# Attention scores of a two-block forward pass: from one f32 product to two f32r products over rounded halves

## The reference

```python
h = rms_norm(x, norm_mix_w[layer]); proj = h @ w_in[layer]
q_nsa = rope(...); k_slc = rope(kv[:, :, 2], ...); k_win = rope(kv[:, :, 4], ...)
kc = gelu(blk(k_cmp) @ w1) @ w2                      # 15 compressed keys for each group
s_cmp = einsum('bshgd,bchd->bhgsc', qg, kc) * scale  # masked softmax, times compressed values
s     = einsum('bqhgd,bhqnkd->bhgqnk', qb, kg) * scale   # selected blocks
s_win = einsum('bnqhgd,bnkhd->bnhgqk', qb, kb) * scale   # window
o = g[..., 0:1] * o_cmp + g[..., 1:2] * o_slc + g[..., 2:3] * o_win
```

## Time and profile before

| what | value |
|---|---|
| median of 3 runs | 1285.89 us (1285.88 to 1286.3) |
| time of the profiled execution | 1286.23 us |
| its span in the trace | 1284.9 us |
| PE busy | 1273.1 us, 99% of the span |
| DVE, ACT, POOL busy | 69%, 53%, 28% |
| share of PE in the chain that ended last | 95% |
| granted clock of PE | 1.00 in every stretch read |

### The profile page before, as it was taken

The page is one execution under the profiler, slowest core; times in us unless marked ns, Lnnn a source line. Parts: engine busy times, 40 slices in busy tenths (PEclk is TensorE's granted clock), DMA queues, the critical chain, the costliest instruction groups (busy, mean ns, idle before and its releaser), DMA issues.

```text
span 1284.9 us, 20030 instructions
## 1 busy us (share of the span) xinstructions
PE 1273.1 (99%) x8220; PEld 1150.0 (90%) x8220; DVE 890.5 (69%) x1309; ACT 686.7 (53%) x985; POOL 356.7 (28%) x268
## 2 busy tenths in 40 slices
PE   8999999999999999999999999999999999999999
PEld 6988889989999879899998888888999998888887
DVE  6775565768888468985567777646898476877752
ACT  6644445466655355466746555435456674655541
POOL 0110021014440059476450000007857733000000
PEclk9999999999999999999999999999999999999999
DMA  9653233555555546734364555544854444555551
GB/s 353 252 193 135 99 116 136 193 183 194 175 188 192 191 147 235 233 134 157 137 212 164 197 183 180 193 164 172 270 196 139 157 157 172 192 174 191 195 186 45
DMA packets 36572, 230.77 MB, mean 180 GB/s; under 512 B 4480, under 2 KB 5120, under 8 KB 10496
## 3 DMA queue, kind: packets, MB, share of 16 engines
q1 hardware_dynamic: 36480, 229.48, 50.9%
HBM read 222.12 MB, written 1.05 MB: 174 GB/s over the span
## 4 chain that ended last, share of the span: by engine, by line
PE 95%; DVE 2%; ACT 1%; DMA 1%; POOL 1%; issue 0%; SPq 0%; DVEq 0%; POOLq 0%
PE ps L601 13%; PE ps L580 12%; PE ps L582 12%; PE ps L581 12%; PE ps L521 11%; PE ps L523 11%; PE ps L522 11%; PE ps L602 7%; PE ps L526 6%; PE ps L540 1%; PE ps L992 1%; PE ps L754 0%; DMA raw<-in_w 0%; POOL sg L1622 0%; DMA gnw<-in_rows 0%
## 5 line engine op out<-in xcount | busy, mean ns | idle before, releaser
L1080 ACT ACTIVATE whi<-raw 128x2048 fp32r<-128x2048 f32 x205 | 390.2, 1906 | 170.9 <-PE ps L523 100.5
L1725 DVE TENSOR_TENSOR wlo<-raw,whi 128x2048 fp32r<-128x2048 f32 (+1 forms) x165 | 380.1, 2307 | 137.7 <-ACT whi L1080 137.1
L580 PE MATMUL ps<-hh,whi 128*128 128x256 f32 x992 | 283.6, 286 | 0.0
L582 PE MATMUL ps<-hh,wlo 128*128 128x256 f32 x992 | 280.6, 283 | 0.0
L581 PE MATMUL ps<-hh,whi 128*128 128x256 f32 x992 | 280.5, 283 | 0.0
L601 PE MATMUL ps<-hh,whi 128*128 128x512 f32 x704 | 249.3, 399 | 0.0
L1601 POOL TENSOR_TENSOR wlo<-raw,whi 128x512 fp32r<-128x512 f32 x160 | 203.8, 1306 | 135.5 <-ACT whi L1080 132.4
L602 PE MATMUL ps<-hh,wlo 128*128 128x256 f32 x704 | 197.7, 281 | 0.0
L581 PEld LDWEIGHTS ps<-hh,whi 128*128 128x128 f32 x992 | 190.1, 192 | 0.4 <-issue 0.2
L580 PEld LDWEIGHTS ps<-hh,whi 128*128 128x128 f32 x992 | 190.0, 192 | 0.4 <-issue 0.2
L582 PEld LDWEIGHTS ps<-hh,wlo 128*128 128x128 f32 x992 | 190.0, 192 | 0.0
(11 more groups left out here) (304 smaller groups left out, 2088.6 us busy)
## 6 DMA issues: line engine op xcount, KB each, us to landing
raw<-in_w SPq DMA_DIRECT2D x203, 1024.0 KB, 4.8
raw<-in_w SPq DMA_DIRECT2D x8, 256.0 KB, 6.4
kst<-kh SPq DMA_DIRECT2D x16, 128.0 KB, 2.4
qst<-qh SPq DMA_DIRECT2D x16, 128.0 KB, 2.3
raw<-in_w SPq DMA_DIRECT2D x2, 560.0 KB, 15.9
x<-in_x SPq DMA_DIRECT2D x2, 512.0 KB, 4.9
gain<-in_rows SPq DMA_DIRECT2D x2, 512.0 KB, 10.2
kst<-kl SPq DMA_DIRECT2D x8, 128.0 KB, 2.4
```

Source lines behind the costliest of these rows:

```text
L580: pe.op.matmul(o, wh[:, k, c:c + 128], hi[:, k, :], start=first, stop=False, skip_group_check=True)
L582: ins = pe.op.matmul(o, wl[:, k, c:c + 128], hi[:, k, :], start=False, stop=last, skip_group_check=True)
L1080: act.op.activation(t.whi[i % NHI][:, 0:n], t.raw[i % NRAW][:, 0:n], ACT.Copy).then_inc(*at("act_hi", ("hi", i)))
L1725: dve.op.tensor_tensor(t.wlo[i % NRAW][:, c], t.raw[i % NRAW][:, c], t.whi[i % NHI][:, c].bitcast(F32), ALU.subtract).then_inc(*at("dve_lo ...
```

## The change

Queries and keys are rounded to f32r halves. For each head the 64 upper rows of the queries stand over the 64 lower ones (`qs`, turned to `q1`); the keys of a group stand twice, one copy above the other (`kd`), turned, and split into `k1h` (upper) and `k1l` (lower). Two f32r products over 128 contraction rows, with `k1h` and with `k1l`, then give all four partial products. The same is done with the compressed keys (`kcs`), where the results of upper and lower keys lie beside each other and DVE adds them. POOL copies the keys twice instead of zeroing `kT`. The weights `w2k` stand twice (64 KB more in a table).

The core of the diff:

```diff
-    ("w2k", 128), ("w2v", 128), ("pe", 32), ("fconv", 4 * 2 * NFT),
+    ("w2k", 256), ("w2v", 128), ("pe", 32), ("fconv", 4 * 2 * NFT),
...
     g = rows("qr", *h)
     steps(g, 5)
-    for tt in range(2):
-        turned(("qT", tt), [("q roped", tt)], t.qkv[tt][:, 0:512], 4)
+    def q_turned(tt):
+
+        src = t.qs[tt][:, :, :, :].rearrange("p h a d -> p (h a d)").bitcast(F32)
+        for h in range(2):
+            turned(("qT", tt, h), [("q lo", tt)], src[:, half(h)], 4)
+
+    q_turned(0)
     run(g)
+    q_turned(1)
...
-    for tt in range(2):
+    def k_turned(tt):
+
         b = take_bank(("kT", tt))
-        pe.wait_ge(*on("k roped", tt))
-        for j in range(2):
-            ins = pe.op.transpose(t.pb[b][:, j * 128:j * 128 + 128], t.qkv[tt][:, 768 + 256 * j:896 + 256 * j], ident)
+        pe.wait_ge(*on("k twice", tt))
+        for gr in range(2):
+            for j in range(2):
+                ins = pe.op.transpose(t.pb[b][:, (2 * gr + j) * 128:(2 * gr + j) * 128 + 128],
+                                      t.kd[tt][:, gr, j, :, :].rearrange("p a d -> p (a d)"), ident)
...
-            product(t.sc[1][gr * 64:gr * 64 + 64, 0:15], w2[0][:, hf, :], t.Hg[:, 0, hf, gr * 15:gr * 15 + 15],
-                    hf == 0, hf == 1, [("kc",)] * (gr + hf == 2))
+            product(t.sc[1][:, gr * 16:gr * 16 + 15], w2[0][:, hf, :],
+                    t.Hg[:, 0, hf, gr * 15:gr * 15 + 15], hf == 0, hf == 1, [("kc",)] * (gr + hf == 2))
...
         product(t.tp[0:120, 0:64], t.Hr[:, hf, :], w2[1][:, hf, :], hf == 0, hf == 1, [("vc",)] * (hf == 1))
+    for tt in range(2):
+        k_turned(tt)
     run(g)
...
-        for b in range(4):
-            product(t.sc[0][:, b * 32:b * 32 + 32], t.qT[:, b, tok(tt)], t.kcT[:, :, :],
-                    names=[("cmp scores", tt)] * (b == 3))
+        for j in range(8):
+            product(t.sc[0][:, j * 32:j * 32 + 32], t.q1[:, j, tok(tt)], t.kcs[:, :, j % 2, :],
+                    names=[("cmp scores", tt)] * (j == 7))
...
-        product(bk[:, :].rearrange("p (a k) -> p a k", a=2)[:, :, 0:n], t.qT[:, b, tok(tt)], t.kT[:, gr, :, 0:n],
-                True, False)
+        for k in t.k1h, t.k1l:
+            product(bk[:, :].rearrange("p (a k) -> p a k", a=2)[:, :, 0:n], t.q1[:, 2 * b + gr, tok(tt)],
+                    k[:, gr, :, 0:n], k is t.k1h, False)
...
+    for tt in range(2):
+        upper(("q hi", tt), t.qs[tt][:, :, 0, :], t.qkv[tt][:, 0:512].rearrange("p (h d) -> p h d", h=8), ("q roped", tt))
     act.wait_ge(*on("gates copied", 1))
...
+    for tt in range(2):
+        lower([("q lo", tt)], t.qs[tt][:, :, 1, :], t.qkv[tt][:, 0:512].rearrange("p (h d) -> p h d", h=8),
+              t.qs[tt][:, :, 0, :], ("q hi", tt))
     run(rows("qr", rotated("qr")))
...
+    for tt in range(2):
+        lower([("free", ("kT", tt))], t.k1l[:, :, :, tok(tt)],
+              bank(("kT", tt))[:, :].rearrange("p (g a s) -> p g a s", g=2, a=2), t.k1h[:, :, :, tok(tt)],
+              ("k hi", tt))
     run(g)
...
         for gr in range(2):
-            dve.op.tensor_tensor(t.cs[:, gr * 4:gr * 4 + 4, :],
-                                 t.sc[0][:, 0:128].rearrange("p (b g c) -> p b g c", g=2, c=16)[:, :, gr, 0:15],
-                                 bc(madd, [128, 4, 15], 1), ALU.add).then_inc(
+            s = t.sc[0][:, 0:256].rearrange("p (b g a c) -> p b g a c", g=2, a=2, c=16)[:, :, gr, :, 0:15]
+            part = t.cs[:, gr * 4:gr * 4 + 4, :]
+            dve.op.tensor_tensor(part, s[:, :, 0, :], bc(madd, [128, 4, 15], 1), ALU.add).then_inc(*at("dve_small"))
+            await_own()
+            dve.op.tensor_tensor(part, s[:, :, 1, :], part, ALU.add).then_inc(
                 *at("dve_small", *([("cmp masked", tt)] * gr)))
```

More of the change, by code:

```diff
@@ L314, in place @@
     t.qkv = [at(f"qkv{i}", n0 + 5.25 * i, [128, 1304]) for i in range(2)]
-    t.qT = at("qT", n0 + 10.5, [128, 4, S])
-    t.kT = at("kT", n0 + 30.5, [128, 2, 2, S])
-    t.Ex = [at(f"Ex{i}", (n0 + 16.5, n0 + 18.5, n0 + 80)[i], [128, 2, S]) for i in range(3)]
+    t.qs = [at(f"qs{i}", n0 + 41 + (12, 20)[i], [128, 8, 2, 64], R32) for i in range(2)]
+    t.kd = [at(f"kd{i}", n0 + (14.5, 26.5)[i], [128, 2, 2, 2, 64]) for i in range(2)]
+    t.q1 = at("q1", p, [128, 8, S], R32)
+    t.k1h, t.k1l = (at(n, n0 + a, [128, 2, 2, S], R32) for n, a in (("k1h", 10.5), ("k1l", 30.5)))
+    t.Ex = [at(f"Ex{i}", n0 + (16.5, 18.5, 14.5)[i], [128, 2, S]) for i in range(3)]
     t.ET = [at(f"ET{i}", n0 + 20.5 + 2 * i, [128, 4, 128]) for i in range(2)]
@@ L713, in compressed @@
     def compressed(tt):
-        pe.wait_ge(*on("qT", 0))
-        pe.wait_ge(*on("qT", 1))
-        pe.wait_ge(*on("kcT"))
+        for k in range(2):
+            pe.wait_ge(*on("free", ("qT", k, 1)))
+        pe.wait_ge(*on("kc lo"))
         if tt:
             pe.wait_ge(*on("exp", 6))
-        for b in range(4):
-            product(t.sc[0][:, b * 32:b * 32 + 32], t.qT[:, b, tok(tt)], t.kcT[:, :, :],
-                    names=[("cmp scores", tt)] * (b == 3))
+        for j in range(8):
+            product(t.sc[0][:, j * 32:j * 32 + 32], t.q1[:, j, tok(tt)], t.kcs[:, :, j % 2, :],
+                    names=[("cmp scores", tt)] * (j == 7))
         yield
@@ L1215, in act_program, with q_turned_out @@
     steps(g, 5)
-    for tt in range(2):
-        turned_out(("qT", tt), t.qT[:, :, tok(tt)])
+    def q_turned_out(tt):
+        for h in range(2):
+            turned_out(("qT", tt, h), t.q1[:, 4 * h:4 * h + 4, tok(tt)])
+    q_turned_out(0)
     run(g)
+    q_turned_out(1)
     def ret_turned(w, tt):
@@ L1230, in act_program @@
             *at("act_small", ("gelu", kv)))
-    run(rows("kr"))
+    g = rows("kr")
+    steps(g, 1)
+    upper(("kc hi",), t.kcs[:, 0, :, 0:15], t.sc[1][:, 0:32].rearrange("p (g c) -> p g c", g=2)[:, :, 0:15], ("kc",),
+          ("rest zero",))
+    for tt in range(2):
+        upper(("k hi", tt), t.k1h[:, :, :, tok(tt)],
+              bank(("kT", tt))[:, :].rearrange("p (g a s) -> p g a s", g=2, a=2), ("kT", tt))
+    run(g)
     units = [(tt, hd) for tt in range(2) for hd in range(8)]
@@ L1607, in pool_program @@
         norm_power("n0", tt)
[L1608 to L1612, removed]
+    for tt in range(2):
+        pool.wait_ge(*on("k roped", tt))
+        for gr in range(2):
+            k = t.qkv[tt][:, 768:1280].rearrange("p (j g d) -> p j g d", j=2, g=4)[:, :, gr, :]
+            pool.op.tensor_copy(t.kd[tt][:, gr, :, :, :], bc(k, [128, 2, 2, 64], 2)).then_inc(
+                *at("pool_small", *([("k twice", tt)] * gr)))
     for w in ("qr", "kr"):
@@ L1948, in dve_program @@
         splits(i + AHEAD)
[L1949 to L1953, removed]
     kr = UNITS["kr"]
@@ L1962, in dve_program @@
             *at("dve_small", *([("Hr",)] * hf)))
-    for gr, rows_of in enumerate(groups):
-        copied([("kcT",)] * gr, t.kcT[rows_of, gr, 0:15], t.sc[1][rows_of, 0:15], ("kc",), ("rest zero",))
+    lower([("kc lo",)], t.kcs[:, 1, :, 0:15], t.sc[1][:, 0:32].rearrange("p (g c) -> p g c", g=2)[:, :, 0:15],
+          t.kcs[:, 0, :, 0:15], ("kc hi",))
     splits(kr[1])
@@ L2561, in _small @@
     put("bm", (np.arange(120)[:, None] // 15 == np.arange(8)[None, :]).astype(f))
-    put("w2k", a["cmp_w2_k"][0].reshape(2, 128, 64).transpose(1, 0, 2))
+    put("w2k", np.tile(a["cmp_w2_k"][0].reshape(2, 128, 1, 64), (1, 1, 2, 1)).transpose(1, 0, 2, 3))
     put("w2v", a["cmp_w2_v"][0].reshape(2, 128, 64).transpose(1, 0, 2))
```

7 lines of the change are left out of this document (3 added, 4 removed).

## The result

The change made the kernel slower: median 1290.66 us (1290.31 to 1291.9, 6 runs) against 1285.92 us (1285.87 to 1286.3, 6 runs), a ratio of 1.0035 with a 95% interval of 1.0025 to 1.0045, or +4.7 us. The prediction said +2.6, and its range of 1285.3 to 1290.7 holds the result by 0.04 us. The profiled execution took 1290.9 us, its span is 1289.6. What is in the profile of after stands two or more lines lower in the program: L542 turns blocks, L523 to L525 are `mul3`, L739 turns `cp`, L768 the probabilities.

The account below looks back on a forecast made before the run. PE, busy 99% of the span, was taken to set the end. Gain -3.9, added work +1.7 and waits +4.75 made +2.6 us: 1288.8 us, or 1288.5 against the median; 8-in-10 range 1285.3 to 1290.7.

Parts of the forecast that it names:

- rival 2: DVE slips: POOL's key copies slow the queries' subtraction, which ends 2.8 us late; sum +5.4, 1291.3 us; chance 10%.
- The gain in the scores: Heads' scores on PE get cheaper, 0.19 us each in the first token tile, 0.40 in the second; 3.9 us in all.
- The last two heads pay nothing: Heads 14 and 15, second tile: shorter scores only lengthen PE's wait behind DVE, by 0.8 us.
- More work on PE: Eight more query transposes +0.9 us, four more key transposes +0.4, wider compressed keys' product +0.4; sum +1.7 us.
- (A): After `qr`, PE waits to turn the second tile's queries until DVE frees the `qr` banks; 2.85 us (2.0 to 3.4).
- (B): The second tile of `vr0` takes a bank of `kr`, and PE waits for DVE's rotation there; 0.9 us.
- (C): Two more dependent DVE operations in the compressed softmax make `cp` 0.5 us later per token tile; +1.0 us (0.5 to 1.2).
- What I cost at nothing: Queries' halves on ACT and DVE, ACT's added copies, POOL's key copies, 64 KB more table: taken as covered, no cost.
- Rivals 1, 3 and 4: 1: bank waits small, 1284.7 us, 10%; 3: products no cheaper, 1301.3 us, 3%; 4: faster still, 1283.0 us, 6%.
- The 131 ns: Skill's spacing of 512-column products, set aside for the trace's 0.23 us; by it the sum would be 1.2 us lower.
- the sum of the waits: New waits of PE at the `qr` banks, the `kr` bank and `cp`, added as 2.85 + 0.9 + 1.0 = 4.75 us.

Follow-up runs that it names:

- the f32 variant: Changed kernel with one f32 product a head in place of the two f32r products, lower halves of the keys left out; 1294.02 us, ratio 1.006.
- the zeroes: Changed kernel with 19 and 8 products of zeroes put into PE's waits ahead of two groups of query transposes; 1289.59 us, ratio 1.0026.
- both spreads: Later projections' steps spread otherwise among the attention's: in the changed kernel with queries and keys moved and additions reordered, 1298.2 us; in the kernel before, 1297.58 us.

## Why the prediction was right, and where it was not

It was right on the sign, and the places and sizes of the waits are nearly all as it said. That the result lies inside its range is luck: 0.04 us from the end, outside the forecast's own range of 1286.9 to 1289.9, and brought that near to the end by a cost that the prediction did not have. Its landing near rival 2 is a coincidence.

- *The gain in the scores*, -3.9 us: measured -1.46 and -2.29, 3.75 together; the f32 variant gives 3.7 back. 0.24 and 0.47 us to the mask were foretold as 0.24 to 0.32 and 0.46 to 0.54.
- *The last two heads pay nothing*: right; the tail's wait went from 0.80 to 1.40, and leaving out their second product brought 0.03. Only what the longer wait does to the clock was not seen.
- *More work on PE*, +1.7: the transposes and the keys' part took about 1.6 (0.88 and 0.68).
- *(A)*, 2.85: in the two pieces and from the releaser named. The view lists 2.68 us of idle time; counted as the prediction counted, from product to product, it is 3.04. *(B)*, 0.9: 0.92, and gone with the move that should remove it.
- *(C)*, 1.0: 0.67 by leaving the additions out. In the second tile 0.51, as said; in the first, where I assumed no slack, 0.16. This term was mis-sized.
- *What I cost at nothing*: the queries' subtraction took 1.49 us for two at 48.79, and DVE stood idle 0.79 us behind it, so that (A) came no later for it; the table is free; ACT's added copies held nobody. POOL's weren't free: where they run, DVE's rotary step is 0.32 us longer, and ACT's splits, DVE's splits and the rotation of `qr` follow it, so that (A) is about 0.2 us longer. That is rival 2 in small and on other operations than it named; that POOL is the reason is inferred from the overlap in time and from the ten and four profiles, and no kernel without the copies was run. The slip that rival 2 priced, 2.8 us, did not happen. Rivals 1, 3 and 4 are refuted by the rows of (A) and of the scores.
- *The 131 ns* that the Trainium skill states for products of 512 columns ("TensorE: Matmul & The Clock Gate", "Back-to-back issue gap"): the two scores' products stand 0.24 us apart (148.76 and 149.00), so the measurement was the right one to take.

The step that failed is the sum of the waits, which priced (A) at its idle time and nothing more: "2.85 + 0.9 + 1.0 = 4.75 us". Behind it PE ran at half clock for 3.4 us, which cost 1.5 us (0.35 in the transposes, 1.19 in `cmpk`). Put beside the profiled execution: 0.43 for the start, 0.13 up to the last product of `qr`, 3.04 + 0.88 + 0.35 in (A), 1.29, 0.68, 0.92, 0.30, -1.46, 0.51, -2.29 make 4.8, against 4.7 us measured. By the prediction's terms, the gain, the added work and the three waits come to 2.4 us where it said 2.6; the half clock adds 1.5, the chance at the start 0.4, and refilling PE behind the waits the rest.

That the half clock comes of PE's idle time is shown by removing the wait (gone), by filling it (gone), and by putting the wait alone into the kernel before (there). Single profiles don't carry that alone, so I count them: of six with the full wait four had the half clock there (after, the f32 kernel, the one without heads 14 and 15's second product, the wait alone) and two not; of eight without it, or with it filled, none (before, the table, the zeroes, the three kernels with moved queries, both spreads). In the two spreads it came behind five of six other waits of 1.5 to 3.9 us. The counts over all executions point the same way, more weakly: the mean clock rounds to 1.000, which leaves no room for a full stretch of half clock anywhere, in 5 of 36 executions with the wait and in 16 of 42 of the four kernels of the change that had it moved or filled. That mean holds the half clocks at the start and behind the last heads too; the kernel before, with no such wait, has 1.000 in 33 of 61. What decides in a single execution stays open. The Trainium skill ("TensorE: Matmul & The Clock Gate", "Part 1: The HAM clock gate (the "warmup" mystery)") says that the hardware's look at PE's activity runs freely and isn't reset by the kernel's start, and that the moment at which the clock changes depends on where in it the first product lands. If the same holds for a wait, it would fit two identical waits with different ends; no run here shows it.

## What to carry to other kernels

A wait on the engine that sets the end can cost more than its length: for each new wait on PE, add what the work behind it would lose at half clock (here 1.4 to 3.2 us), with a chance and not as a certainty, and look in a second profile before believing the first. When a change moves transposes to where their banks are read late, look first whether they can stand one chunk later. Here that, with the keys put back, made good all that the change had lost. Work saved in front of a wait that another engine sets buys nothing and makes the wait longer.

## What the runs showed of the hardware

- The same waits of 2.08 and 0.60 us were followed by a granted clock of 0.53 over 3.4 us in one execution and by 1.00 in another. A wait of 3.19 us was followed by 1.5 us at the full clock, and then by 3.4 us at 0.51.
- A wait of 1.40 us at the last heads, in a stretch with other short gaps, was followed in one execution by 6.8 us at 0.50, for 3.2 us of time. Of eight profiles with a wait of 1.4 to 1.6 us there, two had a half clock behind it and six the full one.
- Waits of 3.92, 2.28 and 2.31 us in one execution (the spread with the change) were each followed, 1 to 1.5 us after PE had started again, by 3.4 us at 0.50 or 0.51.
- At the start, too, the clock fell from one execution to another. It was 0.53 between 11 and 14 us in the kernel before with the spread and 1.00 in the kernel before, whose programs are the same up to there. In the kernel with the wider table it was 0.50 to 0.57 between 9 and 14 us; `cmpk` then started 1.1 us later than in the kernel before, and the execution ended 0.9 us later than that kernel's median.
- Two small VectorE operations that read two tiles of SBUF took 0.35 and 0.38 us while GpSimd copied, and 0.23 and 0.18 us in the kernels where it did not.
